# Row norms of two recurrent attention outputs: token-major products, transposes in place of broadcasts, and waits moved to later writers

## The reference, cut to what matters

```python
# hybrid mixer: three branches; the third is gated linear attention (4 heads of 128 values)
log_a = jax.nn.log_sigmoid((g_lr @ gla_gate_w + gla_gate_b).astype(jnp.float32)) / GLA_GATE_NORM
o_gla = gla_attention(heads(gq, GLA_HEADS), heads(gk, GLA_HEADS), heads(gv, GLA_HEADS),
                      heads(log_a, GLA_HEADS)).astype(h.dtype)
o_gla = (rms_norm(o_gla, gla_out_norm) * jax.nn.silu(heads(g_out, GLA_HEADS))).reshape(B, S, -1)
g_a, g_b, g_c = jnp.split(jax.nn.sigmoid(merge), N_BRANCH, axis=-1)
z = g_a * (o_moba @ w_branch_moba) + g_b * (o_nsa @ w_branch_nsa) + g_c * (o_gla @ w_branch_gla)
return z @ w_out
# gated delta rule: 16 value heads of 128
o = chunk_gated_delta_rule(q, k, v, g, beta)
o = o * lax.rsqrt(jnp.mean(o * o, axis=-1, keepdims=True) + RMS_EPS) * norm_w.astype(jnp.float32)
o = o * jax.nn.silu(z.astype(jnp.float32).reshape(bsz, t, GDN_V_HEADS, GDN_HEAD_DIM))
return o.reshape(bsz, t, GDN_VAL_DIM).astype(x.dtype) @ w_out
```

## Time and profile before

| | |
|---|---|
| median of 3 runs | 2063.43 us (2061.92 to 2064.54) |
| profiled execution | 2062.96 us |
| its span | 2060.7 us |
| mean granted TensorE clock | 0.996 |
| TensorE busy | 2000.0 us, 97% of the span |
| VectorE busy | 1420.4 us, 69% |
| ScalarE busy | 1103.6 us, 54% |
| GpSimd busy | 100.3 us, 5% |
| HBM | 340.81 MB read, 168 GB/s over the span |

### The profile page before, as it was taken

The page is one execution under the profiler, slowest core; times in us unless marked ns, Lnnn a source line. Parts: engine busy times, 40 slices in busy tenths (PEclk is TensorE's granted clock), DMA queues, the critical chain, the costliest instruction groups (busy, mean ns, idle before and its releaser), DMA issues. The chain is left out here.

```text
span 2060.7 us, 40787 instructions
## 1 busy us (share of the span) xinstructions
PE 2000.0 (97%) x15262; PEld 1862.2 (90%) x15262; DVE 1420.4 (69%) x2372; ACT 1103.6 (54%) x1798; POOL 100.3 (5%) x190
## 2 busy tenths in 40 slices
PE   8999999999999999999999999999999899999998
PEld 6899899988988899999999999999999899978997
DVE  5678777776696777776668766576658777467665
ACT  5564455555654555554454544464447776546443
POOL 2011000000020000000000000000001422000000
PEclk9999999999999999999999999999999999999999
DMA  9333555554334555555546465555554444335552
GB/s 304 133 123 114 171 202 194 191 164 164 125 115 142 174 194 189 188 193 185 183 155 226 146 200 188 192 171 184 190 179 163 129 141 143 124 135 184 183 188 98
DMA packets 117813, 348.44 MB, mean 169 GB/s; under 512 B 23288, under 2 KB 35912, under 8 KB 117184
## 3 DMA queue, kind: packets, MB, share of 16 engines
q1 hardware_dynamic: 114960, 335.23, 48.8%
q0 software_dynamic: 2736, 11.59, 1.8%
HBM read 340.81 MB, written 5.96 MB: 168 GB/s over the span
## 5 line engine op out<-in xcount | busy, mean ns | idle before, releaser
L2225 PE MATMUL bank<-xhi,whi 128*128 128x256 f32 x3368 | 960.3, 285 | 15.0 <-DVE xlo L1503 5.2
L2226 PE MATMUL bank<-xlo,whi 128*128 128x256 f32 x3368 | 945.1, 281 | 0.0
L2227 PE MATMUL bank<-xhi,wlo 128*128 128x256 f32 x3368 | 944.5, 280 | 0.0
L1492 DVE TENSOR_TENSOR wlo<-raw,whi 128x1024 fp32r<-128x1024 f32 x621 | 733.4, 1221 | 164.8 <-ACT whi L980 163.8
L2225 PEld LDWEIGHTS bank<-xhi,whi 128*128 128x128 f32 x3368 | 637.3, 189 | 32.6 <-issue 8.7
L2226 PEld LDWEIGHTS bank<-xlo,whi 128*128 128x128 f32 x3368 | 637.9, 189 | 5.3
L980 ACT ACTIVATE whi<-raw 128x1024 fp32r<-128x1024 f32 x621 | 621.2, 1046 | 34.3 <-DVE arena L1757 16.5
L2227 PEld LDWEIGHTS bank<-xhi,wlo 128*128 128x128 f32 x3368 | 637.2, 189 | 0.0
L2225 PE MATMUL bank<-whi,hhi 128*128 128x512 f32 x688 | 273.1, 397 | 3.9 <-DVE hlo L1644 1.5
L2227 PE MATMUL bank<-whi,hlo 128*128 128x512 f32 x688 | 271.3, 394 | 0.0
L2226 PE MATMUL bank<-wlo,hhi 128*128 128x512 f32 x688 | 270.5, 393 | 0.0
(11 more groups left out here) (371 smaller groups left out, 1757.7 us busy)
## 6 DMA issues: line engine op xcount, KB each, us to landing
raw<-panels SPq DMA_DIRECT2D x621, 512.0 KB, 4.2
arena<-w_in POOLq DMA_DIRECT2D x2, 2048.0 KB, 10.9
arena<-relay SPq DMA_DIRECT2D x8, 512.0 KB, 4.1
arena<-gains_in POOLq DMA_DIRECT2D x6, 512.0 KB, 4.0
relay<-arena POOLq DMA_DIRECT2D x4, 512.0 KB, 8.1
relay<-arena SPq DMA_DIRECT2D x4, 512.0 KB, 3.2
x<-x_in SPq DMA_DIRECT2D x1, 1024.0 KB, 4.8
arena<-bias_table POOLq DMA_DIRECT2D x8, 128.0 KB, 5.8
```

The source lines that it names most:

```text
L1492: dve.tensor_tensor(wlo[slot][:], raw[slot][:], whi[slot][:].bitcast(F32), ALU.subtract) \
L2225: pe.matmul(dst, w_hi, a_hi, start=start, stop=False, skip_group_check=True)
L2226: pe.matmul(dst, w_hi, a_lo, start=False, stop=False, skip_group_check=True)
L2227: return pe.matmul(dst, w_lo, a_hi, start=False, stop=stop, skip_group_check=True)
```

## The change

1. **Products turned.** In `delta_o` and at OUT_SLOT the two operands of each matmul change places, so that o comes token-major: 128 tokens on partitions, 128 channels along the row.
2. **Sums of squares.** Delta: `delta_o_squared` (new, p=22) on ScalarE squares each 128x128 piece with `accum_out`, which sums it along the row; `delta_o_sums` and its matmuls are gone. GLA: ScalarE squares straight out of PSUM, and VectorE sums with two reductions.
3. **Scaling.** Delta: VectorE multiplies `o_inv` into o in place, two heads at once (`delta_o_scaled`, new), in slots 41, 42 and 44 and, for the last four heads, in head block 2. GLA: ScalarE copies o out of PSUM with `qk_inv` as the scale, eight pieces.
4. **Transposes.** TensorE transposes o itself back to feature-major: two per delta head block, eight per hybrid stage, these at k=33 and no longer k=32. In the delta blocks `h` comes from one instruction, which reads the bank; `second` is gone.
5. **Waits of the hybrid stages.** TensorE's wait for `gsum` goes from k=1 to k=6, and VectorE's gsum chain from `step(0)` to `after(1)`. ScalarE's `tile` returns for t under 20 ahead of its wait for `tile_read`. The Sqrt of `kc_norm` comes ahead of the panel's copy. Level 0 of the linear attention is written into `psq`, and level 1 into `third` and `conv`, so the wait for the last `o_sum` goes from level 0 to level 1. In slot 47 neither `hi_to` nor `lo_to` is called.

```diff
-        level_q = [third[:, :, :], psq[:, 0, :].rearrange("p (a b) -> p a b", a=2)]
-        level_k = [conv[:, :, :], psq[:, 1, :].rearrange("p (a b) -> p a b", a=2)]
+        level_q = [psq[:, 0, :].rearrange("p (a b) -> p a b", a=2), third[:, :, :]]
+        level_k = [psq[:, 1, :].rearrange("p (a b) -> p a b", a=2), conv[:, :, :]]
...
 # POOL, levels
                     elif li == 0:
+                        v("p_ready", NU - 1, NU)
+                    else:
                         v("o_sum", NU - 1, NU)
...
 # ACT, hybrid
+                    if t < FIRST_OUT_GATE:
+                        return
                     v("tile_read", t - tok_tiles(t), n_feat)
...
                         for g in range(2):
                             v("gla_sum", g, 2)
-                            og = o_gla[:, 2 * g:2 * g + 2, :]
-                            act.activation(og, bank[6 + g][:].rearrange("p (a t) -> p a t", a=2), ACT.Copy) \
-                                .then_inc(y["gla_copied"], 1)
-                            v("gla_copied", g, 2)
-                            act.activation(sq[:, 2 * g:2 * g + 2, :], og, ACT.Square).then_inc(y["gla_squared"], 1)
+                            act.activation(sq[:, 2 * g:2 * g + 2, :], bank[6 + g][:].rearrange("p (a t) -> p a t", a=2),
+                                           ACT.Square).then_inc(y["gla_squared"], 1)
                     if k == OUT_SLOT + 1:
...
+                        v("gla_norm", GLA_STEPS.index("gla_inv"), len(GLA_STEPS))
+                        for g in range(2):
+                            for i in range(4):
+                                last = act.activation(o_gla[:, 2 * g + i // 2, chunk(i % 2)], bank[6 + g][:, chunk(i)],
+                                                      ACT.Copy, scale=qk_inv[:, 4 * g + i:4 * g + i + 1])
+                            last.then_inc(y["gla_scaled"], 1)
 
                 for t in range(TILES):
-                    hi_to(p0 + t + 3)
+                    if t == FIRST_GLA + 3:
+                        v("kc_norm", KC_STEPS.index("kc_ms"), len(KC_STEPS))
+                        act.activation(cmp_ms, cmp_ms, ACT.Sqrt).then_inc(y["kc_norm"], 1)
+                    if t < TILES - 1:
+                        hi_to(p0 + t + 3)
...
 # ACT, delta
+            def delta_o_squared(n):
+                act.wait_ge(d["o_copied"], 2 * (n + 1))
+                for i in range(SET * CHUNKS):
+                    at = SET * CHUNKS * n + i
+                    if at >= 4:
+                        act.wait_ge(d["o_squared"], at - 3)
+                    act.activation(psq[:, 0, i % 4 * P:(i % 4 + 1) * P],
+                                   o_pair(KSET * n + i // 4)[:, i % 4 * P:(i % 4 + 1) * P], ACT.Square,
+                                   accum_out=o_square[:, at:at + 1]).then_inc(d["o_squared"], 1)
...
 # DVE, delta
-                    dve.wait_ge(d["o_rows"], f + 1)
-                    dve.scalar_tensor_tensor(out=second[:, sl, :], in0=o_head(f), scalar=col(("out_norm", s)),
-                                             in1=bank[6 + sl][:, 0:S], op0=ALU.mult, op1=ALU.mult) \
-                        .then_inc(pair_read, 1)
...
+                if kind == DELTA:
+                    dve.wait_ge(d["o_turned"], f + 1)
+                    dve.scalar_tensor_tensor(out=h[:, sl, :], in0=bank[6 + sl][:, 0:S], scalar=col(("out_norm", s)),
+                                             in1=gated, op0=ALU.mult, op1=ALU.mult).then_inc(h_done, 1)
...
+            def delta_o_scaled(pairs):
+                for pair in pairs:
+                    nk = 2 * CHUNKS
+                    by = o_pair(pair).rearrange("p (i e) -> p i e", i=nk)
+                    dve.wait_ge(d["o_inv"], 1 if pair < 3 * KSET else 2)
+                    dve.wait_ge(d["o_copied"], pair + 1)
+                    dve.tensor_tensor(by, by, o_inv[:, nk * pair:nk * (pair + 1)].rearrange("p (i o) -> p i o", o=1)
+                                      .to_broadcast([P, nk, P]), ALU.mult).then_inc(d["o_scaled"], 1)
...
 # PE, delta head blocks
-                        pe.wait_ge(d["o_inv"], 1 if f < 3 * SET else 2)
...
+                        pe.wait_ge(d["o_scaled"], f // 2 + 1)
+                        if f >= 2:
+                            pe.wait_ge(h_done, first_block[s] + f - 1)
...
                         for c in range(CHUNKS):
-                            i = CHUNKS * f + c
-                            last = pe.matmul(bank[6 + f % 2][:, c * P:(c + 1) * P],
-                                             o_inv[:, i:i + 1].to_broadcast([P, P]), ident, start=True, stop=True)
-                        last.then_inc(d["o_rows"], 1)
+                            last = pe.transpose(bank[6 + f % 2][:, c * P:(c + 1) * P],
+                                                o_head(f)[:, c * P:(c + 1) * P], ident)
+                        last.then_inc(d["o_turned"], 1)
...
 # PE, hybrid
-                    if k == OUT_SLOT + 1:
+                    if k == OUT_SLOT + 3:
                         for i in range(8):
-                            last = pe.matmul(bank[2 + i // 4][:, chunk(i % 4)], qk_inv[:, i:i + 1].to_broadcast([P, P]),
-                                             ident, start=True, stop=True)
+                            if i % 4 == 0:
+                                v("gla_scaled", i // 4, 2)
+                            last = pe.transpose(bank[2 + i // 4][:, chunk(i % 4)], o_gla[:, i // 2, chunk(i % 2)], ident)
```

More of the change, by code:

```diff
@@ L552, in build @@
             "inverse_t_out "
-            "l16_sum l16 l32_sum l32 t32 l64_sum l64 new_sum new v1_in o_sum o_copied o_squared o_sums o_added o_root o_inv o_rows").split()}
+            "l16_sum l16 l32_sum l32 t32 l64_sum l64 new_sum new v1_in o_sum o_copied o_squared o_added o_root o_inv o_scaled o_turned").split()}
         x_loaded = sem("x_loaded")
@@ L648, in acts_before, with pairs_before @@
             return sum(n_blocks(t) for t in range(s) if stages[t][0] in (FFN1, FFN2, DELTA))
+        def pairs_before(s):
+            return sum(n_blocks(t) for t in range(s) if stages[t][0] != DELTA)
         def products_before(s):
@@ L1786, in step @@
                         dve.tensor_copy(cmp_rows, bank[0][:, 0:P]).then_inc(y["cmp_bias"], 1)
-                        v("low_gate", GATE_STEPS.index("gate_ln"), len(GATE_STEPS))
-                        link(dve.scalar_tensor_tensor(out=third[:, :, :], in0=gsum, scalar=0.0, in1=conv[:, :, :],
-                                                      op0=ALU.min, op1=ALU.subtract))
-                        for a in range(2):
-                            dve.tensor_tensor_scan(gsum[:, a, :], ones_row, third[:, a, :], 0.0, ALU.mult, ALU.add) \
-                                .then_inc(y["gsum"], 1)
-                        v("low_tanh", 0, 1)
-                        g = lowrank[ROW_G:ROW_G + 3 * HEADS, :]
-                        dve.tensor_scalar(g, g, 0.5, 0.5, ALU.mult, ALU.add).then_inc(y["gsum"], 1)
                     if k == 1:
@@ L1909, in step @@
                     if k == OUT_SLOT + 1:
-                        v("gla_norm", GLA_STEPS.index("gla_sums"), len(GLA_STEPS))
-                        dve.tensor_scalar(qk_ms[:, 0, 0:8], bank[0][:, 0:8], 1.0 / P, EPS, ALU.mult, ALU.add) \
+                        for g in range(2):
+                            v("gla_squared", g, 2)
+                            last = dve.tensor_reduce(qk_ms[:, 0, 4 * g:4 * g + 4],
+                                                     sq[:, 2 * g:2 * g + 2, :].rearrange("p a (c e) -> p (a c) e", c=CHUNKS),
+                                                     AX.X, ALU.add)
+                        link(last)
+                        dve.tensor_scalar(qk_ms[:, 0, 0:8], qk_ms[:, 0, 0:8], 1.0 / P, EPS, ALU.mult, ALU.add) \
                             .then_inc(y["gla_norm"], 1)
@@ L2445, in step @@
                         v("cmp_attn", CMP_STEPS.index("cmp_p"), len(CMP_STEPS))
+                        v("gsum", 0, 3)
                         for i in range(8):
@@ L2815, in delta_o @@
                         last.then_inc(d["o_sum"], 1)
-            def delta_o_sums(n, groups):
-                if n + 2 < SETS:
-                    pe.wait_ge(d["norm_ms"], 2 * (n + 3))
-                for g in groups:
-                    pe.wait_ge(d["o_squared"], 2 * n + g + 1)
-                    for hh in range(2):
-                        for c in range(CHUNKS):
-                            i = CHUNKS * (2 * g + hh) + c
-                            o = hh * S + c * P
-                            last = pe.matmul(bank[3][:, i:i + 1], psq[:, 0, o:o + P], ones[:, 0:1],
-                                             start=True, stop=True)
-                    last.then_inc(d["o_sums"], 1)
             def delta_step(s, n, o):
```

113 lines of the change are left out of this document (55 added, 58 removed).

## The result

The changed kernel takes 2040.38 us (median of 4, 2039.86 to 2041.18), the kernel before beside it 2063.98; the ratio is 0.9888, interval 0.9871 to 0.9905. The forecast was 2044.6 in a range of 2035 to 2056. The span of the profiled execution went from 2060.7 to 2038.6 us, 22.1 less.

What follows compares the result with a forecast made beforehand. TensorE was taken as the bound, busy 2000.0 of 2060.7 us, with VectorE binding mid-hybrid-stage. Gains 6.6 + 1.4 + 1.6 + 4.7 + 4.5 = 18.8 from 2062.96 gave 2044.2, 2044.6 on the median, range 2035 to 2056.

Steps and rivals of the forecast that it cites:

- the likeliest case: Whole kernel: the summed forecast of 2044.6 us on the median, own range 2039 to 2050, chance 0.62.
- d: Delta, slots 23 to 39: row sums of squares leave TensorE, 5.8 us off, less 1.1 for ScalarE's copies; gain 4.7.
- a: Start of the hybrid stages: waits at gsum, the Gelu and the step after go; gain 3.3 per layer, 6.6.
- the 0.3 for a late chain: Start of the hybrid stages: moved gsum chain delays tile reads of k=2 and 3, taking back 0.3 us per layer.
- b: Level 0 of the linear attention: TensorE's wait for POOL's first level goes; gain 0.7 per layer, 1.4.
- c: GLA output in the merge tail: removed TensorE work mostly becomes waits in a 2.99 us loop; gain 0.8 per layer, 1.6.
- the term of 1.1 for ScalarE's copies: Delta slots 23 to 39: ScalarE's added squares make its copies for the next set late, losing 1.1 us.
- e: Delta's end: nothing gained, the path runs through ScalarE and VectorE; first down product at 1803.6 where it was 1803.36.
- f: The 16 head blocks: second leaves VectorE's loop, a block takes 3.06 us instead of 3.57; gain 4.5.
- nothing takes the place: Whole kernel: rival that all removed TensorE work and waits count, 29.0 us, giving 2034.4; chance 0.13.
- The hybrid stages give nothing: Hybrid stages: rival that VectorE's load bounds them, leaving only 9.2 us from the delta parts, 2054.2; chance 0.17.
- The clock rival: 18 places with transposes: rival that the granted clock falls behind each, 1.7 us apiece, 31 us, 2075; chance 0.04.

Runs made afterwards that it cites:

- e10: Changed kernel with VectorE's gsum chain back in step(0), ahead of the panel's split, TensorE's wait staying at k=6: 2047.15 us.
- e11: Changed kernel with ScalarE's wait for tile_read put back in the slots under 20: 2043.42 us.
- e2: Kernel before with the GLA output's part of the change alone: 2063.35 us, ratio 1.0.
- e1: Kernel before with part 5 of the change alone (the waits of the hybrid stages): 2051.33 us, ratio 0.9944.
- e12: Changed kernel with the splits (hi_to, lo_to) called in slot 47 again on both engines: 2042.37 us.
- e3: Kernel before with the delta stage's part of the change alone: 2052.37 us, ratio 0.9949.
- e4: Changed kernel with 48 unread row-sum matmul records put back at p=22 and p=23 of the first three delta sets: 2044.6 us.
- e9: Changed kernel with the GLA output turned at k=32 instead of 33 (TensorE's transposes and VectorE's last product): 2044.04 us.
- e7: Changed kernel with the last four heads' scaling moved from VectorE to ScalarE, in head blocks 3 and 4: 2039.98 us.
- e8: Changed kernel with the last four heads scaled on ScalarE and the last set's squares made ahead of silu of the last z panel: 2039.05 us.

## Why the prediction was right, point by point

The time came out 4.2 us under the forecast, and inside its range, with the likeliest case as it was described. By the profiled executions the kernel gained 22.1 us where 18.8 were forecast. Part of the nearness is luck: d brought 1.8 less than forecast, and the start of the program (1.1) and the low stretch in part a (1.6), for which no term stood, more than made up for it.

**a** was forecast at 3.3 per layer and measured 3.9, or 5.5 with the low stretch that went with the wait. The size of the removed waits (3.6) was right, the 0.3 for a late chain was not due. The division among the causes was wrong: the chain in front of the split was the larger (e10), ScalarE's wait the smaller (e11).

**b** 0.7 forecast, 0.6 measured in both layers.

**c** 0.8 forecast, 1.0 and 0.5 measured. In layer 1 the lead rose from 7.17 to 8.67 with the low stretch at 166 us gone, rose on to 11.1 as TensorE's matmuls went, and fell back to 8.15 in the tail; in layer 2 it went from 12.6 to 16.1 and back to 13.1. So the tail kept what was removed, as the argument from its 2.99 us said. e2 and e1 show that the GLA output is worth nothing; what c did gain is the guards in slot 47 (0.6 per layer by e12) and the low stretch. The prediction had the guards at about 1 us.

**d** 4.7 forecast, 2.9 measured. The failed step is the term of 1.1 for ScalarE's copies: nothing was lost to them. In its place TensorE waited 1.8 us more for the relay in sets 1 and 3, for which the prediction had no term; by the leads the changed kernel loses 2.7 around these waits, the rest without a named wait. e3 gained 5.3 in the same slots without them.

**e** was forecast as a loss of 0.2 and gained 0.6. The term mis-sized is the square with its sum: 0.39 us from a row with 128x128 behind one of another form, 0.29 measured, 2.35 for eight in place of 3.1.

**f** the block was forecast at 3.06 and measured 3.06; the scaling at f=2 was forecast at 0.4 and costs 0.74. With VectorE ahead, blocks take TensorE's 3.00. The 1.0 by which f did better comes at the end: the lead is 21.07 at the last transposes and 22.05 at the next stage's first.

Of the rivals, "nothing takes the place" would have needed 29 us: e2 refutes it for the GLA part, and blocks of 3.06 us where TensorE needs 3.00 refute it for part of the delta blocks. For the row sums of the delta slots it comes near the truth in e3 (5.3 of 5.8) and not in the changed kernel (2.9). "The hybrid stages give nothing" is refuted by e1, 12.0 us. Transposes cost one record: 32 in 16 blocks. The clock rival said that transposes let the granted clock fall. The granted clock is 1.00 from 1600 to 2030 us, all 16 blocks included, and a block takes 3.00 us for 2.79 of matmuls and two transposes. The Trainium skill ("TensorE: Matmul & The Clock Gate", Part 4: PE-mode transpose) says that transposes do not count as TensorE being busy in the same way. With two among twelve matmuls this case's trace shows no effect of that. But the clock did move the result, by another way than that rival's: behind waits.

## What to carry to other kernels

When work leaves the bounding engine, ask for each place what was hidden under that work. Where a loop over the other engines sets the pace (here 2.99 us a slot), the work that goes only becomes a wait, and the longer wait can bring a low stretch of the clock besides. Read a wait's last releaser together with the program order behind it: the chain in front of the split cost more than the wait that the trace named. And compare timelines at the same instructions, not totals, so that chance in the clock is seen and set apart.

## What the runs showed of the hardware

The same wait in the same code has a low stretch behind it in one program and none in another. TensorE's wait for `h` at the second head block is 1.97 us in the changed kernel and in e12; the next transposes come 3.78 us later in the one (1786.09 to 1789.87, above), and 5.32 in the other. e12:

```profile
1787.40 0.41 PE L2363 MATMUL bank<-masks,arena 128*128 128x128 f32 x2 [1.97 <-DVE h L1662]
...
1792.72 0.38 PE L2363 MATMUL bank<-masks,arena 128*128 128x128 f32 x2
```

A low stretch takes 1.6 us where TensorE sets the pace: e10's distance behind the changed kernel goes from 5.1 to 6.6 at the one in layer 2 and stays there. In the delta head blocks, where VectorE sets the pace, it takes nothing in the end: e4 is 1.8 behind ahead of the blocks, 3.4 behind at the low stretch (1790 us), and 1.8 behind again at the end of the blocks; e9, e10 and e12 do the same. The next one, at 1845 us, takes 0.9 in e4, e9 and e10.

From 20 to 2000 us the profiled executions had four low stretches in before, two in the changed kernel, eight in e2. The mean granted clock is 0.9937 over the 33 runs of before beside the experiments and 0.9968 over the four of the changed kernel. That is at most some 6 us (0.0031 x 2050) of the gain of 23.6, since a low stretch does not always cost its time, and the forecast had no term for it. A difference of 2 us between two programs can be this alone, and e7 and e8 could not be ordered by their times. ScalarE squares 128x128 with the sum read out every 0.293 us (32 squares, 9.4 us busy).
